# A gated convolution and neighbourhood-attention layer: value products moved into the next pair, V's second part loaded by GpSimd, and new orders at the start and the end of the pairs

## The reference, cut to what matters

```
h = rmsnorm(x) * norm_g
a, glu, z_a, q, k, v, z_b, g_a, g_b = split(h @ w_in)          # nine blocks of 1024 columns
u = a * sigmoid(glu)
c = depthwise_conv(u, width 31) + dw_b
y_a = (silu(layernorm(c)) * silu(z_a)) @ w_pw_a
s = q . k / 8 + bias(head, dr, dc), window of 8 rows x 16 columns on a grid 64 wide
o = softmax(s) @ v                                             # 16 heads of 64
y_b = (o * silu(z_b)) @ w_o_b
m = sigmoid(g_a + b) * y_a + sigmoid(g_b + b) * y_b
y = rmsnorm(x + m @ w_out) * final_g
```

## Time and profile before

| | |
|---|---|
| median of 3 runs | 1743.12 us (1741.56 to 1745.41) |
| profiled execution | 1739.94 us, span 1738.1 us |
| TensorE busy | 1726.1 us (99%), 8604 matmuls |
| VectorE, ScalarE, GpSimd busy | 1162.3 (67%), 466.8 (27%), 200.2 us (12%) |
| chain that ended last | TensorE 89%, DMA 5%, VectorE 2% |
| HBM traffic | 247.56 MB, mean 142 GB/s |

### The profile page before, as it was taken

The page is one execution under the profiler, slowest core; times in us unless marked ns, Lnnn a source line. Parts: engine busy times, 40 slices in busy tenths (PEclk is TensorE's granted clock), DMA queues, the critical chain, the costliest instruction groups (busy, mean ns, idle before and its releaser), DMA issues.

```text
span 1738.1 us, 24594 instructions
## 1 busy us (share of the span) xinstructions
PE 1726.1 (99%) x8604; PEld 1405.8 (81%) x8604; DVE 1162.3 (67%) x1797; ACT 466.8 (27%) x925; POOL 200.2 (12%) x251
## 2 busy tenths in 40 slices
PE   9999999999999999999999999999999999999998
PEld 7888877788888888888888888888877888888886
DVE  6549255897689489579669948976985755335332
ACT  5411133123122122222222222221334344102222
POOL 1110011011011011101101100210110064000001
PEclk9999999999999999999999999999999999999999
DMA  8751345545435625634543453463467765543223
GB/s 296 244 93 49 94 110 142 157 121 158 127 86 168 169 50 145 173 84 125 167 126 97 133 164 90 121 167 111 115 171 282 256 208 175 192 133 110 74 91 127
DMA packets 299177, 247.56 MB, mean 142 GB/s; under 512 B 117815, under 2 KB 252999, under 8 KB 298988
## 3 DMA queue, kind: packets, MB, share of 16 engines
q1 hardware_dynamic: 246666, 153.04, 32.2%
q10 hardware_dynamic: 48578, 79.97, 13.3%
q0 software_dynamic: 3872, 13.75, 3.2%
HBM read 158.78 MB, written 87.90 MB: 142 GB/s over the span
## 4 chain that ended last, share of the span: by engine, by line
PE 89%; DMA 5%; DVE 2%; SPq 1%; ACT 1%; issue 1%; ACTq 0%; POOL 0%; POOLq 0%; DVEq 0%
PE pg L1523 71%; PE pg L1541 12%; PE pO L1638 3%; PE pS L1621 3%; DMA raw<-in_w_in 1%; DMA x_d<-work 1%; DMA work<-p_d 1%; DMA work<-tb_d 1%; SPq L528 1%; ACT xs L867 0%; DMA p_d<-work 0%; SPq L464 0%; DMA c_d<-work 0%; DVE work L1298 0%; ACT work L764 0%
## 5 line engine op out<-in xcount | busy, mean ns | idle before, releaser
L1523 PE MATMUL pg<-xs,ws 128*128 128x512 f32 x5688 | 1312.0, 391 | 0.8 <-DVE work L1419 0.5
L1523 PEld LDWEIGHTS pg<-xs,ws 128*128 128x128 f32 x5688 | 1062.1, 188 | 232.9 <-issue 11.4
L1214 DVE SCALAR_TENSOR_TENSOR work<-work 128x1551 f32<-128x1551 f32 x240 | 438.5, 1827 | 4.6
L1541 PE MATMUL pg<-ws,xs 128*128 128x512 f32 x1008 | 237.0, 393 | 0.7 <-DVE xs L1157 0.7
L1541 PEld LDWEIGHTS pg<-ws,xs 128*128 128x128 f32 x1008 | 190.4, 189 | 41.6 <-DVE ws L1108 1.0
L680 POOL TENSOR_TENSOR work<-work 128x384 f32<-128x384 bf16 (+1 forms) x72 | 62.3, 866 | 981.1 <-DVE small L1286 968.3
L1286 DVE CUSTOM_DVE_ANT_0 work<-pS,work 128x384 f32<-128x384 f32 (+1 forms) x192 | 88.4, 510 | 114.7 <-PE pS L1621 113.9
L955 ACT ACTIVATE work<-work,small 128x384 f32<-128x384 f32 (+1 forms) x192 | 109.2, 570 | 156.0 <-DVE small L1286 156.0
L1108 DVE TENSOR_TENSOR ws<-raw,ws 128x1024 fp32r<-128x1024 f32 x89 | 110.2, 1239 | 38.5 <-ACT ws L733 38.5
L733 ACT ACTIVATE ws<-raw 128x1024 fp32r<-128x1024 f32 x89 | 93.5, 1053 | 126.3 <-PE pg L1523 98.6
L1298 DVE STREAM_TRANSPOSE work<-work 128x384 f32<-128x384 f32 (+1 forms) x192 | 102.6, 534 | 6.6
(11 more groups left out here) (111 smaller groups left out, 905.8 us busy)
## 6 DMA issues: line engine op xcount, KB each, us to landing
raw<-in_w_in SPq DMA_DIRECT2D x70, 512.0 KB, 4.6
p_d<-work SPq DMA_DIRECT2D x256, 96.0 KB, 2.1
work<-p_d ACTq DMA_DIRECT2D x64, 384.0 KB, 5.1
work<-v_d SPq DMA_DIRECT2D x128, 96.0 KB, 2.7
p_d<-work SPq DMA_DIRECT2D x128, 64.0 KB, 1.9
work<-p_d ACTq DMA_DIRECT2D x32, 256.0 KB, 4.4
v_d<-work ACTq DMA_DIRECT2D x24, 256.0 KB, 2.1
za_d<-work ACTq DMA_DIRECT2D x24, 256.0 KB, 2.1
```

The costliest lines, as they stand in the source:

```text
L1214: nc.vector.scalar_tensor_tensor(cv[:, 0:CLEN], u[:, k:k + CLEN], cur[:, k:k + 1], cv[:, 0:CLEN], ALU.mult, ALU.add).then_inc(tap_ok, 1)
L1523: last = nc.tensor.matmul(pg[b][:], wt(s, wpart)[:, k * P:(k + 1) * P], xs[:, k, xpart, chunk(n)], start=(k == 0 and wpart == 1), stop=(k ...
L1541: last = nc.tensor.matmul(pg[b][:], xs[:, k, xpart, t * P:(t + 1) * P], wt(s0 + k // 2, wpart)[:, chunk(k % 2)], start=(k == 0 and xpart = ...
```

## The change

- Pairs: gate A goes ahead of z_B in the middle pairs and in the last one. The value products of the last two blocks of pairs 0 to 6 move into slot 1 of the next pair, behind its first scores; the product with z_B (`take_last_o`) into slot 2, the store of `tb` into slot 3.
- V: its row groups 0 and 1 are loaded by SP as before, once the first four blocks' products are done; groups 2 to 5 by GpSimd (16 loads of 64 KB) ahead of its tiles of kind 4 in the next pair, with a semaphore `vr_in` that the products of block 4 wait for.
- Start: `norm_g` is turned into a column `gcol`, tile 0 is scaled by the root only, and `norm_g` goes in with the high and low part, now in eight pieces of 128x128. GpSimd takes the low part of the first weight piece. The first two groups are interleaved by hand (`first_groups`). Square sums, turns, the load of `norm_g` and the load of the masks (three shuffles earlier, by code order after shuffle 7) change places; `xn` gets two places apart.
- End of pair 7: SP loads the stored pair tiles only when all probabilities are back, and the second `w_o_b` piece behind five of them; each tile has its own semaphore; the first refill goes in the order 3, 4, 5, 2, 6, 7, 0, 1; VectorE's first gate stands behind three of the eight operations of the third refill.

```diff
-UNIT = (T_ZB, T_ZA, T_GA, T_GB, T_A, T_GLU, T_Q, T_K)
-LAST_UNIT = (T_ZB, T_ZA, T_GA, T_GB, T_GA2, T_GB2)
+UNIT = (T_GA, T_ZB, T_ZA, T_GB, T_A, T_GLU, T_Q, T_K)
+LAST_UNIT = (T_GA, T_ZB, T_ZA, T_GB, T_GA2, T_GB2)
+TB_ORDER = (3, 4, 5, 2, 6, 7, 0, 1)
-VALUE_SLOTS = (7, 13, 19, 25, 31, 37)
+VALUE_SLOTS = (7, 13, 19, 25, 31)
-FIRST_VALUES = (8, 13, 18, 23, 28, 32)
+FIRST_VALUES = (8, 13, 18, 23, 28)
...
+        def load_v(eng, i, groups, landed):
+            v4 = v_d.rearrange("(g r t) d -> r t g d", g=6, r=4)
+            for j in range(4):
+                for r in range(4):
+                    src = v4[r, BAND_START[j]:BAND_START[j] + BAND, groups, bass.ds(i * P, P)]
+                    eng.dma_start(vb[BAND * r:BAND * r + BAND, groups, j, :], src).then_inc(landed, 16)
...
-            for t in range(NT - 5, NT):
-                shuffle_x(t)
+            shuffle_x(7)
             sp.wait_ge(w_lo, 4)
             sp.dma_start(msk32, masks).then_inc(mask_in, 16)
+            for t in range(8, NT):
+                shuffle_x(t)
...
                 sp.wait_ge(tb_out, 16 * (PAIRS - 1))
                 sp.wait_ge(qk_done, BLK * PAIRS)
+                for n in range(2):
+                    sp.wait_ge(p_in[n], 96 * PAIRS)
                 load_tb(3)
...
-                        load_v(i + 1, BLOCKS * i + BLOCKS)
+                        sp.wait_ge(pv_done, BLOCKS * i + 4)
+                        load_v(sp, i + 1, slice(0, 2), v_in)
...
-            piece_y(S_YB + 1)
-            for n in range(2):
-                sp.wait_ge(p_in[n], 96 * PAIRS)
             sp.wait_ge(bias_ok, 18 * PAIRS)
             load_tb(5)
...
             load_tb(6)
+            piece_y(S_YB + 1)
             sp.wait_ge(pv_done, BLOCKS * PAIRS)
...
+                if t == 1:
+                    pool.wait_ge(w_hi, 1)
+                    pool.wait_ge(xn_ok, 2)
+                    nc.gpsimd.tensor_tensor(wt(0, 1), raw_of(0), wt(0, 0).bitcast(F32), ALU.subtract).then_inc(w_lo, 1)
...
                 for kd in range(KINDS):
+                    if kd == 4 and not (isinstance(i, int) and i == 0):
+                        pool.wait_ge(pv_done, BLOCKS * i)
+                        load_v(pool, i, slice(2, 6), vr_in)
...
+                if t == 0:
+                    act.wait_ge(gc_ok, 1)
+                    for k in range(4 * hf, 4 * hf + 4):
+                        nc.scalar.activation(xs[:, k, 0, 0:P], pH[k // 2][:, k % 2 * P:(k % 2 + 1) * P], ACT.Copy,
+                                             scale=gcol[:, k:k + 1]).then_inc(x_hi if k % 4 == 3 else x0_hi, 1)
+                    return
...
+                    if slot == 3 and not first:
+                        act.wait_ge(o_out, NCH * i)
+                        act.dma_start(row_of(tb_d, i - 1), tb).then_inc(tb_out, 16)
...
-                        dve.wait_ge(ng_ps, hf + 1)
                         x = xt[:, 0, chunk(hf)]
-                        nc.vector.scalar_tensor_tensor(x, x, rstd[:, 0:1], pS[hf][:], ALU.mult, ALU.mult).then_inc(xn_ok, 1)
+                        nc.vector.tensor_scalar(x, x, rstd[:, 0:1], None, ALU.mult).then_inc(xn_ok, 1)
...
+                    if slot == 2 and tiles is not FIRST_UNIT:
+                        take_last_o()
...
                 if last:
-                    refill_tb(2)
+                    refill_tb(2, range(3))
...
+            gate(0)
+            refill_tb(2, range(3, KT))
...
+            def first_groups():
...
+                by_hi(0)
+                by_hi(1)
+                by_lo(0)
+                by_hi(2)
+                by_lo(1)
+                h_t(1)
+                by_hi(3)
+                by_lo(2)
+                pe.wait_ge(x_hi, 3)
+                passes(1, range(4), 0, 0)
+                by_lo(3).then_inc(g_done, 1)
...
+                    if b == 4:
+                        after(pe, vr_in, 256 * i)
...
+                    if slot == 1 and tiles is not FIRST_UNIT:
+                        values(BLOCKS - 2, True)
+                        values(BLOCKS - 1, True)
```

200 lines of the change are left out of this document (137 added, 63 removed).

## The result

The changed kernel takes 1754.87 us (median of six runs, 1754.22 to 1756.11) against 1743.53 for the kernel before (1741.56 to 1745.41): ratio 1.0068, interval 1.0057 to 1.0079. It is 11.3 us slower, where the forecast was 3.9 faster. Its profiled execution has a span of 1754.3 us.

What follows compares the result with a forecast made beforehand. TensorE, busy 1726.1 of 1738.1 us, was taken as the bound, so only its idle or slow stretches could be won. 1.2 + 0.26 + 0.79 + 1.49 + 0.77 - 0.3 - 0.3 = 3.9 us gave 1739.2; range 1736.0 to 1743.5.

Steps and rivals of the forecast that it cites:

- The base of the sum: Whole kernel: the 3.9 us gain, worked out on the profiled execution (1739.94 us), taken equally off the median, 1743.12.
- The start: First token groups: matmuls begin earlier and denser, at 9.2 us; gain 1.2 us, ends 0 and 1.9.
- 99.89, 0.26: GLU tile: masks issued three shuffles earlier bring weights sooner; TensorE's 0.26 us wait goes and the start's 1.2 passes.
- End of pair 0, 0.79: End of pair 0: 0.79 us of waiting for probabilities goes, the value visit standing over three groups later.
- Pair 7's values, 1.49: End of pair 7, value visit: probabilities land alone as SP waits for them first; gain 1.49 us, bounds 0 and 1.49.
- The refill, 0.77 less 0.3: End of pair 7: VectorE's earlier gate gains 0.77 us; ScalarE's later copies lose 0.3, bounds 0 and 2.2.
- The loop's order, 0.3: Loop pairs, third scores: gate tile first leaves z_A evacuations thin margins; cost 0.05 us per pair, 0.3 in all.
- V on GpSimd, 0: Loop pairs: sixteen V loads issued by GpSimd take 9.6 us; cost 0 while a cover of 6 us holds.
- Rival 2: Loop: GpSimd's issues block VectorE's tensor_scalars, up to 0.6 us each; costs 3.9 us, time 1743.1; chance 0.10.
- a wait for a bank in the loop: Loop: TensorE waiting anywhere for a bank was named as a sign of being wrong at the root.
- Rival 3: Loop: GpSimd can't issue sixteen loads in a row; TensorE idles 2.6 us in 6 pairs, time 1754.8; chance 0.06.
- Rival 1: Start and end of pair 7: gains given back, 2.0 us, by late pair tiles or weight piece; time 1741.2; chance 0.23.

Runs made afterwards that it cites:

- Experiment 12: The kernel before, unchanged, run again for a second profiled execution: span 1744.0 us, 5.9 more than the first profile; that execution took 1745.88 us.
- experiment 4: Changed kernel with turns behind the low parts, the end's loads in old order and V's second part loaded by SP: 1747.81 us.
- the one with four parts undone: Changed kernel with turns behind the low parts, masks behind the last shuffle, end's loads in old order, V's second part by SP: 1743.07 us, ratio 1.000.

## Why the prediction was wrong, step by step

The steps that failed, by the starts in the changed kernel against the first profile of the kernel before (us won, forecast and measured): the start and the GLU tile, 1.46 forecast and 10.0 lost (4.2 lost against the second profile); the first refill, 0.47 forecast and 5.2 lost; the value products of pair 7, 1.49 forecast and 0.9 lost. The end of pair 0 won 1.0 (0.79 forecast), the loop lost 0.9 (0.3 forecast). These make up 16.0.

- **The base of the sum.** I took the profiled execution's 0.26 us at 99.89 for the kernel's state, and carried the sum over to the median with the same amount. The profile lay 3.2 us below the median, and I left that as it was. Experiment 12 shows that this wait isn't fixed: an execution 2.7 us above the median waits 2.7 us there and loses 1.6 more to the clock. What the median execution does there, no trace shows. The fast profile overstates the change's loss too: 16.2 us by the two profiles, 11.3 by the medians.
- **The start, 1.2.** Near as far as it was worked out, and in part by luck: first matmul at 9.27 (9.2 forecast), token group 2 at 1.03 us sooner than in the first profile. But the matmuls come at 0.23 already from about 11, not from 14.5 or 15.4, and TensorE then waits 1.36 us for the third weight piece (to 13.91; 13.7 forecast), so that piece and not the clock sets the gain. And in four other executions with the start of the kernel before, token group 2 begins at 25.1, not 25.7: against them the changed start wins 0.4. The step that failed is the tacit one that the rest of the start would follow. The section on the change says that turns, square sums and loads change places; the prediction never costed it: a `turn` of 2.9 us more ahead of an `h_lo` that TensorE waits for, and a square sum that holds up the turn in front of it. A wait of 4.1 us and 3.0 us of lower clock came of it, and four shorter waits of 3.1 in all.
- **99.89, 0.26.** The wait did go, and the weights came sooner. But I asked only who stands behind the masks in their old place, not who stands behind them in the new one: the writes of tiles 8 to 11, each with a reload behind it (four shuffles, where the section on the change and the prediction say three). In the changed kernel this was hidden by the turns; on its own it costs 5.4 to 6.5 us of wait.
- **End of pair 0, 0.79.** Right, slightly more: pair 1 starts 9.0 us late instead of 10.0.
- **Pair 7's values, 1.49.** The last visit is without a wait, as forecast; from the 36 matmuls ahead of it to the run behind it are 9.88 us, 11.22 before, so 1.34 won. The first visit waits 1.92 us, which no step had, and of which 1.3 go when SP loads V instead of GpSimd (0.61 in experiment 4). Net a loss of 0.9 over pair 7 (9.94 late at its second scores, 10.87 at the first matmul behind it).
- **The refill, 0.77 less 0.3.** The second term was mis-sized, and outside its bounds of 0 to 2.2: the stretch from the first w_o_b matmul to the variances took 66.50 us before, 71.67 after. The mechanism that I had priced, ScalarE's evacuation behind its copies, cost 1.0 us; the other 4.4 (a wait of 2.77 and 1.6 of lower clock) came by a path that no step had, from the refill over GpSimd's loads of `c_d` to VectorE and its gate. I had named the piece behind five loads and ScalarE before it, and put the last copies near 1330; ScalarE began the first at 1340.01. A load of 512 KB behind five of 768 KB landed after 14.6 us, not after the few that I gave it.
- **The loop's order, 0.3.** The edge is where I put it: z_A(0) and z_A(1) are taken at 388.54 and 394.48, the forecast's 379.51 and 385.46 and the 9.0 by which the pair is late. But on no margin TensorE loses 0.2 to 0.25 a pair (16.87 us for the 72 matmuls in pair 1, 16.66 before), not 0.05. About 0.2 a pair come back elsewhere, since the six pairs lose 0.9 in all, 0.7 of it by V (below); that the merged value visit gives it is likely, but not shown.
- **V on GpSimd, 0.** The sixteen issues took 8.94 us (9.6 forecast) and nothing waited for V, but the loads cost 2.4 us by experiment 4, where the forecast had nothing. Rival 2's mechanism, issues that hold up VectorE's tensor_scalars, doesn't show: the longest beside the issues is 0.81 us, as in the kernel before. What slowed VectorE were GpSimd's two tiles, which the issues had pushed beside a tap, for 0.35 us of TensorE in each of two pairs; that is also a wait for a bank in the loop, which the prediction had named as a sign of being wrong at the root. Rival 3 gives the measured time, 1754.8, by a mechanism that did not happen: the issues had no wait in their midst.
- **Rival 1**, gains given back at both ends, names both places. Its price (2.0) is too small because it stopped at giving back.

The ledger that the medians give: of 11.8 us between the changed kernel and the one with four parts undone (1754.87, 1743.07), 4.2 are the end's order, 2.4 are V on GpSimd, and 5.2 are the start (4.7 of them seen when the masks alone go back, after the turns; that step compares two groups of measurements whose kernels before differ by 1.1, and set against these it is 5.9). What is left of the change gains nothing that can be told from zero. What the moved square sum costs by itself was not varied. What stays open, too, is how much of the varying round trip is due to the DMA traffic beside it; no run varied that alone.

## What to carry over

When a load is moved forward in a queue, list what now stands behind it, and follow the longest round trip among these. Where several limits end at about the same time, undo changes in pairs too: singly each will look free. And where the profiled execution is faster than the median, look for a margin of tenths of a microsecond in it before taking its waits as the kernel's: here the same wait was 0.26 us in one execution, and 2.70 with 1.6 of lower clock in another.

## What the runs showed of the hardware

- What a wait of TensorE costs on top, by matmuls at the 1.2 GHz level behind it, is not fixed by its length. The wait of 4.09 us in the token groups cost 3.0, 2.4, 2.5 and 1.7 in four executions. Also there, 2.25 and 2.46 us cost nothing, 2.27 cost 1.6 (96 matmuls in 23.61 us, where 22.05 is usual; granted clock 0.79 from 60 to 68), 5.45 cost 1.5, 6.01 cost 2.6, 6.45 cost 2.0. At the GLU tile 2.24 and 2.70 cost 1.6, 2.26 cost 2.8. At the gate of w_o_b 2.72 and 2.77 cost 1.6, 2.54 and 3.00 nothing. At the first value visit of pair 7 1.65 and 1.79 cost 1.6, 1.92 and 1.94 nothing.
- Sixteen loads in a row from GpSimd took 8.94 us to issue, 0.56 each, without a stall.
- A tap on VectorE (two SBUF inputs) went from 1.83 to 3.68 us with two GpSimd operations of 0.93 beside it, though by the timeline the tap had begun first; GpSimd's kept their 0.93.
- The reloads of the shuffled tiles followed each other by 5.2 to 6.4 us in one execution of the kernel before (from 41.20 to 69.27) and by 5.5 to 6.8 in another (42.18 to 72.97), with the same instructions.
